# Expert products of a mixture layer as plain float32 matmuls on four column quarters of the array

## The reference

```python
logits = t @ w_router                              # t: tokens x 1024
top_v, top_i = lax.top_k(logits, 2)
gates = one_hot(top_i) weighted by softmax(top_v)
for e in range(8):
    gate, up = split(t @ w_gu[e], 2)               # w_gu[e]: 1024 x 7168
    out += gates[:, e:e+1] * ((silu(gate) * up) @ w_down[e])   # w_down[e]: 3584 x 1024
```

## Time and profile before

| what | value |
|---|---|
| median of 3 runs | 1658.79 us (1658.18 to 1662.62) |
| span of the profiled execution | 1656.5 us |
| TensorE busy (matmuls) | 1611.3 us, 97% |
| VectorE, ScalarE busy | 1291.2 us (78%), 1001.0 us (60%) |
| expert stage, first to last product | from 668.9 to 1635.3 us of the span |
| DMA over the span | 425 MB, mean 257 GB/s |

### The profile page before, as it was taken

The page is one execution under the profiler, slowest core; times in us unless marked ns, Lnnn a source line. Parts: engine busy times, 40 slices in busy tenths (PEclk is TensorE's granted clock), DMA queues, the critical chain, the costliest instruction groups (busy, mean ns, idle before and its releaser), DMA issues.

```text
span 1656.5 us, 30082 instructions
## 1 busy us (share of the span) xinstructions
PE 1611.3 (97%) x12174; PEld 1272.0 (77%) x12174; DVE 1291.2 (78%) x1274; ACT 1001.0 (60%) x1043; POOL 127.5 (8%) x148
## 2 busy tenths in 40 slices
PE   8999999999999998999999999999999999999997
PEld 6779999959889977777776776777777777777775
DVE  4766555487844476898998998998998998998996
ACT  4755443346422235777776777777777777776774
POOL 3330001200035412000000000000000000000000
PEclk9999999999999999999999999999999999999999
DMA  9533546514300012699999999999999999999991
GB/s 258 204 125 127 177 177 230 180 39 143 112 4 4 4 50 88 242 369 374 358 364 374 357 371 371 356 368 374 357 367 372 359 366 372 358 369 371 359 371 52
DMA packets 60916, 425.42 MB, mean 257 GB/s; under 512 B 6999, under 2 KB 8135, under 8 KB 10104
## 3 DMA queue, kind: packets, MB, share of 16 engines
q1 hardware_dynamic: 58776, 416.52, 66.6%
q0 software_dynamic: 2016, 7.13, 1.8%
HBM read 422.28 MB, written 1.12 MB: 256 GB/s over the span
## 4 chain that ended last, share of the span: by engine, by line
PE 74%; DVE 2%; issue 1%; ACT 1%; POOL 0%; ACTq 0%; DVEq 0%
PE PS L569 56%; PE PS L899 6%; PE PS L570 5%; PE PS L1150 1%; PE PS L918 1%; PE PS L1080 1%; PE PS L927 1%; DVE arena L1524 1%; PE PS L625 0%; PE PS L1113 0%; PE PS L1114 0%; PE PS L890 0%; PE PS L1016 0%; PE PS L833 0%; PE PS L883 0%
## 5 line engine op out<-in xcount | busy, mean ns | idle before, releaser
L1524 DVE TENSOR_TENSOR w_lo<-ring,w_hi 128x2048 fp32r<-128x2048 f32 x391 | 896.0, 2293 | 174.0 <-ACT w_hi L1451 86.0
L1451 ACT ACTIVATE w_hi<-ring 128x2048 fp32r<-128x2048 f32 x334 | 641.0, 1919 | 264.2 <-PE PS L569 239.0
L569 PE MATMUL PS<-w_hi,x_hi 128*96 128x512 f32 x896 | 353.8, 395 | 0.7 <-ACT x_hi L1443 0.7
L569 PE MATMUL PS<-w_hi,x_lo 128*96 128x512 f32 x896 | 352.5, 393 | 0.0
L569 PE MATMUL PS<-w_lo,x_hi 128*96 128x512 f32 x896 | 243.0, 392 | 0.0
L1217 ACT ACTIVATE w_hi<-ring 128x2048 fp32r<-128x2048 f32 x55 | 105.3, 1915 | 157.2 <-issue 83.9
L569 PEld LDWEIGHTS PS<-w_lo,x_hi 128*96 128x96 f32 x896 | 144.6, 161 | 62.1
L569 PEld LDWEIGHTS PS<-w_hi,x_lo 128*96 128x96 f32 x896 | 144.8, 162 | 58.4
L569 PEld LDWEIGHTS PS<-w_hi,x_hi 128*96 128x96 f32 x896 | 144.6, 161 | 57.9 <-ACT x_hi L1443 1.0
L569 PE MATMUL PS<-w_hi,hid_hi 128*96 128x512 f32 x444 | 175.1, 394 | 0.0
L569 PE MATMUL PS<-w_hi,hid_lo 128*96 128x512 f32 x444 | 174.5, 393 | 0.0
(11 more groups left out here) (290 smaller groups left out, 2060.5 us busy)
## 6 DMA issues: line engine op xcount, KB each, us to landing
ring<-in_slabs SPq DMA_DIRECT2D x394, 1024.0 KB, 4.8
arena<-in_lora POOLq DMA_DIRECT2D x1, 1152.0 KB, 5.4
h<-in_h SPq DMA_DIRECT2D x2, 544.0 KB, 5.6
arena<-bias_lines POOLq DMA_DIRECT2D x1, 1056.0 KB, 20.9
arena<-bias_lines POOLq DMA_DIRECT2D x1, 1040.0 KB, 26.3
ring<-in_slabs SPq DMA_DIRECT2D x4, 256.0 KB, 8.3
arena<-in_lora POOLq DMA_DIRECT2D x1, 1024.0 KB, 12.3
out<-h SPq DMA_DIRECT2D x4, 256.0 KB, 2.2
```

Of the source, the lines that this page charges most:

```text
L569: return pe.matmul(out, x, w, start=start, stop=stop) if tokens_stay else \
L1451: act.activation(w_hi[:, n % 2, :], ring[:, n % SLOTS, :], ACT.Copy).then_inc(hi_set, 1)
L1524: tt = lambda o, a, b, op=ALU.mult: dve.tensor_tensor(out=o, in0=a, in1=b, op=op)
```

## The change

In the expert stage the weights are no longer rounded and split. Each slab is multiplied straight from the ring as plain float32. The array is used as four column quarters of 32 columns: each takes 32 of the 96 tokens as stationary operand and writes to its own 32 partitions of PSUM. Three quarters take the three token blocks with 3/4 of the features (three blocks of 128 columns of 512, or of 256 columns of 1024), the fourth takes the remaining quarter of the features, for the three token blocks in turn. So a piece of 512 columns becomes 12 matmuls of 128 columns, a piece of 1024 columns 12 matmuls of 256, and a slab 48 matmuls (gate and up) or 24 (down). The slot is released when TensorE has used the slab (`slab_used`). Gathered tokens are kept once (`x_all`), ScalarE and VectorE taking turns, and so is the hidden layer (`hid_T`): three transposes of 128 x 128 a group in place of four of 96 x 128. An expert's outputs of the fourth quarter lie on partitions 96 to 127 and are first moved by three small ScalarE copies (`y_side`). The two early slabs (`EARLY`) and `products_by_half` go.

```diff
+X_BANK = [4, 5, 0, 1, 2, 3, 6, 7]
-EARLY = 2
+BLK = 32
+BLOCKS = CAP // BLK
+MAIN = BLOCKS * P
+OUT_MAIN, OUT_SIDE = 768, 256
...
+            more_slabs(SLOTS, SL_MOE + SLOTS, slab_taken)
+            more_slabs(SL_MOE + SLOTS, N_SLABS, slab_used)
...
             def gather(o):
 
+                def rows_of(j, rows, first):
+                    half, k = divmod(j, KC)
+                    for t in range(TT):
+                        mm = pe.matmul(PS[:, X_BANK[j % 8], 0:HALF], rows[:, t, P * k:P * k + P],
+                                       pick[:, t, 4 * half:4 * half + 4, :].rearrange("p e c -> p (e c)"),
+                                       start=first and t == 0, stop=not first and t == TT - 1)
+                    return mm
+
                 pe.wait_ge(hn_hi_set, TT * o + TT)
...
                 def hidden_transposed(g):
                     pe.wait_ge(rows_set, GROUPS * q + (g + 1))
...
-                    for j in range(GROUP // P):
-                        mm = pe.transpose(PS[:, 4 + g % 2, CAP * j:CAP * (j + 1)],
-                                          hid_rows[0:CAP, g % 2, P * j:P * (j + 1)], eye[0:CAP, 0:CAP])
+                    for i in range(BLOCKS):
+                        mm = pe.transpose(PS[:, 4 + g % 2, P * i:P * (i + 1)],
+                                          hid_rows[:, g % 2, P * i:P * (i + 1)], eye[:, :])
                     mm.then_inc(hidT_ps, 1)
 
+                def four(k, bank, col, w, w_main, w_side, width, first, last):
+
+
+                    for i in range(BLOCKS):
+                        for j in range(BLOCKS + 1):
+                            at = w_main + width * i if j < BLOCKS else w_side
+                            b, c = bank(i), col(i)
+                            mm = pe.matmul(PS[BLK * j:BLK * (j + 1), b, c:c + width], k(j if j < BLOCKS else i),
+                                           w[:, at:at + width], start=first and c == 0, stop=last,
+                                           skip_group_check=True)
+                    return mm
...
+                    pe.wait_ge(loaded[n % SLOTS], 96 * q + 16 * (n // SLOTS + 1))
+                    w = ring[:, n % SLOTS, :]
                     if g < GROUPS:
                         if part == 0 and g >= 2:
                             pe.wait_ge(rows_set, GROUPS * q + (g - 1))
-                        out = PS[0:CAP, 2 * (g % 2) + part // 2, :]
-                        pieces = [(k % 4, x_hi[:, k, at], x_lo[:, k, at], out, k == 0, k == KC - 1)
-                                  for k in range(4 * (part % 2), 4 * (part % 2) + 4)]
+                        for c in range(4):
+                            k = 4 * (part % 2) + c
+                            mm = four(tokens(k), lambda x: 2 * (g % 2) + part // 2, lambda x: P * x, w,
+                                      GROUP * c, GROUP * c + MAIN, P, k == 0, k == KC - 1)
...
+                        pe.wait_ge(hidT_kept, GROUPS * q + ((f + 1) * P // GROUP + 1))
+                        for c in range(2):
+                            mm = four(hidden(f + c), lambda x: 6 + x // 2, lambda x: OUT_SIDE * (x % 2), w,
+                                      D * c, D * c + OUT_MAIN, OUT_SIDE, f + c == 0, f + c == FTE - 1)
+                    mm.then_inc(slab_used, 1)
...
-            def round_expert_slab(q, i):
-                n = SL_MOE + i
-                act.wait_ge(loaded[n % SLOTS], 96 * q + 16 * (n // SLOTS + 1))
-                act.wait_ge(hi_free, SL_EXPERT * q + (n - 1))
-                act.wait_ge(slab_taken, SL_EXPERT * q + (n - 1))
-                act.activation(w_hi[:, n % 2, :], ring[:, n % SLOTS, :], ACT.Copy).then_inc(hi_set, 1)
...
+            def round_out(q, e):
+                act.wait_ge(slab_used, SL_EXPERT * q + (SL_MOE + SL_EXPERT))
+                for i in range(BLOCKS):
+                    c = OUT_SIDE * (i % 2)
+                    a = act.activation(y_side[BLK * i:BLK * (i + 1), :], PS[CAP:P, 6 + i // 2, c:c + OUT_SIDE], ACT.Copy)
+                a.then_inc(y_moved, 1)
+                gate = slot_gate[0:CAP, e:e + 1]
+                act.activation(yn_hi[0:CAP, 0:GROUP], PS[0:CAP, 6, :], ACT.Copy, scale=gate).then_inc(yn_rounded, 1)
+                act.activation(yn_hi[0:CAP, GROUP:OUT_MAIN], PS[0:CAP, 7, 0:OUT_MAIN - GROUP], ACT.Copy, scale=gate)
+                act.wait_ge(y_moved, q + 1)
+                act.activation(yn_hi[0:CAP, OUT_MAIN:D], y_side[0:CAP, :], ACT.Copy, scale=gate).then_inc(yn_rounded, 1)
...
-            def split_expert_slab(q, i):
-                n = SL_MOE + i
-                dve.wait_ge(hi_set, SL_EXPERT * q + (n + 1))
-                dve.wait_ge(slab_used, SL_EXPERT * q + (n - 1))
-                tt(w_lo[:, n % 2, :], ring[:, n % SLOTS, :], w_hi[:, n % 2, :].bitcast(F32), ALU.subtract)\
-                    .then_inc(slab_taken, 1)
...
             def split_out(q, e):
-                for i in range(2):
-                    at = slice(GROUP * i, GROUP * (i + 1))
-                    dve.wait_ge(yn_rounded, 2 * q + (i + 1))
...
+                dve.wait_ge(yn_rounded, 2 * q + 1)
+                low(slice(0, GROUP), PS[0:CAP, 6, :]).then_inc(yn_split, 1)
+                dve.wait_ge(yn_rounded, 2 * q + 2)
+                low(slice(GROUP, OUT_MAIN), PS[0:CAP, 7, 0:OUT_MAIN - GROUP])
+                low(slice(OUT_MAIN, D), y_side[0:CAP, :]).then_inc(yn_split, 1)
```

More of the change, by code:

```diff
@@ L428, in _, with more_slabs @@
                 sp.dma_start(ring[:, j, :], A["slabs"][j, :, :]).then_inc(loaded[j], 16)
[L429 to L437, removed]
+            def more_slabs(first, last, used):
+                whole = -(-first // SLOTS), last // SLOTS
+                for n in range(first, SLOTS * whole[0]):
+                    sp.wait_ge(used, n - SLOTS + 1)
+                    sp.dma_start(ring[:, n % SLOTS, :], A["slabs"][n, :, :]).then_inc(loaded[n % SLOTS], 16)
+                with sp.Fori(*whole) as i:
+                    for j in range(SLOTS):
+                        sp.wait_ge(used, SLOTS * i + (j - SLOTS + 1))
+                        sp.dma_start(ring[:, j:j + 1, :],
+                                     A["slabs"][bass.ds(SLOTS * i + j, 1), :, :].rearrange("s p c -> p s c"))\
+                          .then_inc(loaded[j], 16)
+                for n in range(SLOTS * whole[1], last):
+                    sp.wait_ge(used, n - SLOTS + 1)
+                    sp.dma_start(ring[:, n % SLOTS, :], A["slabs"][n, :, :]).then_inc(loaded[n % SLOTS], 16)
+            more_slabs(SLOTS, SL_MOE + SLOTS, slab_taken)
+            more_slabs(SL_MOE + SLOTS, N_SLABS, slab_used)
             sp.wait_ge(rt_dve, RT_FLAG)
@@ L1064, in gather @@
             def gather(o):
-                pe.wait_ge(hn_hi_set, TT * o + TT)
[L1067 to L1083, removed]
+                def rows_of(j, rows, first):
[5 more added lines that the diff above has]
+                    return mm
+                pe.wait_ge(hn_hi_set, TT * o + TT)
+                pe.wait_ge(picked, 2 * o + 1)
+                for j in range(2):
+                    rows_of(j, hn_hi, True)
+                pe.wait_ge(hn_split, TT * o + TT)
+                for j in range(2):
+                    rows_of(j, hn_lo, False).then_inc(x_ps, 1)
+                for j in range(2, JOBS):
+                    if j == KC:
+                        pe.wait_ge(picked, 2 * o + 2)
+                    if j == 6:
+                        pe.wait_ge(rt_dve, RT_FLAG)
+                    if j >= 8:
+                        pe.wait_ge(x_kept_v if j % 2 else x_kept_a, KC * o + (j // 2 - 3))
+                    rows_of(j, hn_hi, True)
+                    rows_of(j, hn_lo, False).then_inc(x_ps, 1)
             def gates_of_slots(o):
@@ L1172, in expert @@
                                 pe.wait_ge(put_kept, 2 * o + 2)
[L1173 to L1178, removed]
-                        products(SL_EXPERT * q + (SL_MOE + i), (SL_MOE + i) % 2, GROUP, pieces, tokens_stay=True)
+                        pe.wait_ge(hidT_kept, GROUPS * q + ((f + 1) * P // GROUP + 1))
[3 more added lines that the diff above has]
+                    mm.then_inc(slab_used, 1)
                     if e == 0:
@@ L1429, in _ @@
                 act.activation(out_hi[:, k, TEXT], r_[:, k, TEXT], ACT.Copy).then_inc(out_hi_set, 1)
-            for n in range(SL_O2 + 2, SL_MOE + EARLY):
+            for n in range(SL_O2 + 2, SL_MOE):
                 round_slab(n)
@@ L1497, in _ @@
                 with act.Fori(1, PASSES) as i:
-                    for j in range(EARLY):
-                        round_expert_slab(EXPERTS * i, j)
                     round_rows(i)
@@ L1547, in residual @@
                                                      op0=ALU.mult, op1=ALU.add).then_inc(zsum[l], 1)
-                    if base + n + 2 <= SL_MOE and n < slabs - 1:
+                    if base + n + 2 < SL_MOE and n < slabs - 1:
                         split_slab(base + n + 2)
@@ L2021, in _ @@
```

(2 more changed lines are left out.)

114 lines of the change are left out of this document (44 added, 70 removed).

## The result

The changed kernel takes 1796.31 us (median of 4 runs, 1792.21 to 1803.70) against 1659.44 for the kernel before (4 runs): the ratio is 1.0824, 95% interval 1.0795 to 1.0853. It is 8% slower, where 1639 was predicted and 1706 was the upper end. This is the prediction's first rival, and the time lies above even the 1706 to 1776 at which it was priced there.

What follows compares the result with a forecast made beforehand. TensorE was taken to bound the kernel, with VectorE and DMA near their end; 1656.5 - 22.3 (stage) + 2.0 (end) = 1636.2, plus 2.3 for runs, 1638.5, stated as 1639 us; whole range 1622 to 1706.

Steps and rivals of the forecast that it cites:

- the prediction's first rival: The same as rival 1: TensorE not fed with instructions in gate and up slabs, 1706 to 1776 us; chance 0.25.
- The plain matmul: Expert products: two passes per plain float32 matmul, 0.1106 us a pass for 128 columns, 0.216 for 256.
- Quarters side by side: Expert products: four column quarters run at once, a turn of four matmuls costing no more than one.
- Rival 3: Expert products: quarters overlap only in part or their loads show; a quarter of the full 726 us gives 1820; chance 0.10.
- The sum for the new stage: Expert stage: products, transposes, scatters, gates and picks sum to 944.1 us against 966.4, 22.3 less.
- the change of tile shape: Expert stage: leaving the quarters for full-width matmuls and coming back costs 0.32 us, at transposes, scatters, gates and picks.
- the packet distance: Gate and up slabs: time per instruction packet for TensorE, between 3.3 and 4.4 us, deciding near 3.6.
- rival 1: Gate and up slabs: TensorE pauses mid-slab for instruction packets; 1706 us at 4.0 a packet, 1776 at 4.4; chance 0.25.
- Beside the stage: Kernel's end: side copies of 1.2 us and later scatters finish 4.5 us behind the last product, 2.0 us more.
- Hidden work and slots: Expert stage: freeing ScalarE and VectorE gives nothing; slots free one slab later cost 0; DMA does not bind.
- rival 2: Expert stage: slight instruction shortage, 1655 us, or DMA held at its earlier rate, 1659 to 1661; chance 0.13.

Runs made afterwards that it cites:

- quiet: Changed kernel with each expert slab load past the first seven cut to 16 of 2048 columns, all instructions kept; 1633.7 us.
- wide_inter: Changed kernel with gate and up main quarters taking 384 columns in one matmul instead of three of 128, mains and sides in turn; 1632.35 us, 0.9829 to before.
- wide_fill: wide_tail plus five matmuls into a free bank, sums unread, in TensorE's two waits at the end; 1630.68 us, 0.9824 to before.
- wide_tail: wide_inter with ScalarE scaling the first 512 output columns ahead of the three side copies; 1628.81 us, 0.9813 to before.
- small4k: Changed kernel with each expert slab loaded by two DMAs of 1024 columns, packets of 4 KB, same bytes; 1875.33 us, 1.1310 to before.

## Why the prediction was wrong, point by point

**The plain matmul.** Right. Passes cost 0.1106 us for 128 columns and (31.29 - 0.38)/143 = 0.216 for 256, as read from the earlier trace rows; quiet has the first (10.62/96). The row in the changed kernel's timeline that has the second is the 12 last slabs of a down part:

```profile
778.95 31.29 PE L1163 MATMUL PS<-ring,hid_T 128*32 128x256 f32 x576
```

**Quarters side by side.** Right: a turn of four matmuls costs what one costs, 2.655 us a slab in quiet and 2.59 in down slabs, for hundreds of us. Rival 3 did not occur. The rule of the Trainium skill that was weighed with it (TensorE: Matmul & The Clock Gate, Measured speedup vs the span model) does not hold for this form: three column quarters with the same moving data and a fourth with its own lost nothing that these rows show.

**The sum for the new stage.** 944.1 us was the sum without pauses. wide_inter, which has next to none, takes 933.7 (674.47 to 1608.17), quiet 939.3 (667.99 to 1607.24). The 5 to 10 us less are mainly the change of tile shape, which costs less than the 0.32 taken from L792: transposes of a group 0.48 us (838.72 to 839.19) against 0.66, x 56 = 10.1; scatters some 1.14 against 1.26, x 14 = 1.7. Down parts were as predicted.

**The step that failed: the packet distance in rival 1.** The prediction had the mechanism, the places (gate and up only, mid-slab, down slabs safe), the size of a packet and, nearly, the point at which it decides (3.6 us a packet; its 195 records a slab are 193.5, since transposes are recorded once, and the measured point is 3.67). What it got wrong is the distance that it took as likeliest, 3.3 to 3.6, and with it the chance of 0.25 for the rival that occurred. Worked out from the result: 1090.6 less down parts 290.3, transposes 26.9, scatters 16.0 and 4.6 for gates and picks leaves 752.8, or 3.36 us a gate and up slab, 0.71 over 2.65; 224 x 0.71 = 159 us; the stage is 156.9 us longer than wide_inter's. A packet then took (3.36 + 0.12) x 256/193.5 = 4.60 us, and the packets' own starts say 4.69. That this is near the 4.4 of the earlier trace rows, which the prediction put aside as "partly other waits", is chance: in that window TensorE was busy for 116.67 of 120 us, so 4.4 is how fast it used packets and no sign of how fast they can come.

The rows that argued for the shorter distance came from 460 to 580 us, where slab traffic was all but absent: 13 GB/s in the earlier trace rows. The new need would arise at the 373 GB/s that the prediction worked out. The prediction said that DMA busy with slabs "can only lengthen it" and put no number on it. quiet and the changed kernel give that number: 3.74 us a packet beside 7 GB/s and 4.69 beside 324, 163 us of the kernel's time. Since the need (3.67 us) and the supply without the traffic (3.72) stood side by side, any lengthening had to be felt nearly in full. At the 3.3 us that the rows had suggested, nearly 0.4 us a packet would have been to spare; there was next to nothing.

The Trainium skill (Runtime: NRT & Kernel Launch, Instruction fetch mechanics) says that fetching is hidden because an engine issues slower than the memory is refilled, and that a long kernel need not fit. On the hiding the runs disagree for TensorE: beside the slab traffic these products waited 0.7 us at 96 records a slab, 115 at 192, 312 at 192 with half the columns.

**Beside the stage.** The end was mis-sized: 5.5 us more against 2.0. Three copies of 0.38 us, 1.16 in all, were as taken (1.2), and the last scatter matmul ended 1769.87 - 1763.65 = 6.2 us behind the last product, against a forecast of 4.5. What was missed is the clock. It had been at 1.00 in the last products, TensorE then stood idle 2.77 us, and in the scatter it fell to the lower of its two levels (0.50 from 1766.7 to 1769.7, 1.2 GHz). Timeline of the changed kernel:

```profile
1766.35 0.39 PE L1131 MATMUL PS<-put,sq_rounded 96*128 96x256 f32 x1 [2.77 <-DVE sq_rounded L1982]
...
1767.11 0.41 PE L1131 MATMUL PS<-put,sq_rounded 96*128 96x256 f32 x1
...
1775.80 5.41 PE L637 MATMUL PS<-sq,ones_d 128*128 128x256 f32 x16 [2.30 <-ACT sq L1254]
```

The scatter's matmuls lie 0.21 us apart instead of 0.12 (13 of them, 1.2 us), and L637 takes 5.4 us instead of 3.7. In the one profiled execution of wide_fill, where TensorE was kept at work in both waits, the clock stayed at 1.00; in those of wide_inter and wide_tail it fell.

**Ahead of the stage.** Not predicted: 4.2 us. The stage began at 668.90 before, 673.08 in the changed kernel and 674.47 in wide_inter, but 667.99 in quiet and 668.92 in small4k, whose instructions up to there are those of the changed kernel. Part of it is the clock, at the lower level for longer. Windows of the changed kernel, granted clock third from the end:

```profile
610.00:615.00 5.00, 5.00 (x15) 3.69 (x15) 5.00 (x16) 1.97 (x6) 0.00 (x0) 0.50 0.00 0
615.00:620.00 5.00, 5.00 (x26) 5.00 (x26) 4.42 (x8) 1.01 (x3) 0.00 (x0) 0.52 0.00 0
```

In the kernel before the second of these windows had 1.00. quiet and small4k have 1.00 there too. So it differs between executions of the same instructions; whether the change makes the late start likelier isn't shown.

**Hidden work and slots.** Right: slots that come free one slab later cost nothing. wide_inter moves 372 GB/s in the stage with no wait for a slab, and rival 2's "DMA held at its rate of before" did not occur.

## What to carry to other kernels

Instructions are traffic too. Before cutting matmuls into smaller ones, count records for each 256 and the time that TensorE takes for them, and compare that with the packet distance under the DMA load that the stage will have, not under that of the rows at hand: here a packet came each 3.7 us without slab traffic and each 4.7 beside it, and the kernel needed one each 3.67. Where tiles of the array run side by side, give each as many columns per instruction as its data allow: the same layout with mains of 384 columns turned 8% slower into 1.7% faster than before. And a rival whose deciding point lies inside the spread of the rows, as here 3.6 between 3.3 and 4.4, deserves more than a chance of 0.25, above all if the rows come from a stage without the traffic.

## What the runs showed of the hardware

- The pauses need both instructions and data traffic: 1633.7 us without slabs, 1632.4 with slabs and half the gate and up instructions, 1796.3 with both.
- Slabs in packets of 4 and 2 KB instead of 8 KB, by two and four DMAs a slab, hold the instructions up more, not less: 5.12 and 5.27 us between instruction packets against 4.69, 1875 and 1905 us.
- DMAs of 64 partitions with rows of 8 KB moved 213 GB/s at a DMA share of 0.97, where those of 128 partitions moved 378 at 0.98 (wide_inter, the same window from 700 to 1600).
- A busy quarter doesn't hold up a free one over three instructions: mains of 384 columns first and sides last ran as fast as the two in turn (1631.7 and 1632.4 us).
